# Paired stick-breaking heads, first weights in three pieces with norm sums beside the steps, and linear attention scores in row halves

## The reference, cut to what matters

```python
x += 0.5 * post(SwiGLU_1(pre(x)))          # D_MODEL 1024, D_FF 2816
h  = pre(x) @ w_in                         # GLA q, k, v, gate, low rank | SB q, k, v
# stick-breaking heads (8, dh 64), strictly causal:
z = q k^T / 8 + bias
log_stay = where(valid, log_sigmoid(-z), 0)
after = reverse_cumsum(log_stay) - log_stay
w = where(valid, exp(log_sigmoid(z) + after), 0);  o = w v
# gated linear attention (4 heads, dk 64, dv 128), exact decays between every two tokens
att[t,s] = sum_d q[t,d] k[s,d] exp(b[t,d] - b[s,d]);  o = att v + (q exp(b)) S
x += post(concat(rms(o_gla) * silu(gate), rms(o_sb)) @ w_out)
x += 0.5 * post(SwiGLU_2(pre(x)))
x += post(sigmoid(pre(x) @ W_g) * (p @ W_up))
```

## Time and profile before

| | |
|---|---|
| median of 3 runs | 1417.98 us (1417.67 to 1421.84) |
| the profiled execution's own time | 1419.12 us |
| its span, first to last instruction | 1417.4 us |
| granted TensorE clock, mean share of full | 0.942 |
| busy: PE, DVE, ACT, POOL | 1297.7, 606.0, 412.9, 151.1 us |

### The profile page before, as it was taken

How to read it: one execution, slowest core, us unless ns; L and a number is a source line. 1 busy time by engine, 2 the same in 40 slices (tenths; PEclk the granted TensorE clock), 3 DMA queues, 4 the chain that set the end, 5 groups by cost and what they waited for, 6 DMA issues and landing times.

```text
span 1417.4 us, 22180 instructions
## 1 busy us (share of the span) xinstructions
PE 1297.7 (92%) x9420; PEld 1226.5 (87%) x9420; DVE 606.0 (43%) x631; ACT 412.9 (29%) x462; POOL 151.1 (11%) x167
## 2 busy tenths in 40 slices
PE   5999999999986999979979869589999999999883
PEld 4999999999985999957647649589999999999883
DVE  5344412444337222345467641744442134433744
ACT  5222222222234111244321063432222222222442
POOL 6200000000013000010023301300000000001321
PEclk9999999999997999979967869899999999999997
DMA  5222223222331222211500102112222322222201
GB/s 184 89 89 81 68 89 119 61 88 67 91 109 32 87 89 92 90 47 46 163 30 17 32 16 90 60 58 78 79 78 80 104 90 89 78 75 88 87 31 64
DMA packets 36743, 109.98 MB, mean 78 GB/s; under 512 B 4626, under 2 KB 4642, under 8 KB 36562
## 3 DMA queue, kind: packets, MB, share of 16 engines
q1 hardware_dynamic: 34850, 103.10, 22.3%
q0 software_dynamic: 1232, 5.01, 1.1%
q10 hardware_dynamic: 608, 1.10, 0.2%
HBM read 103.57 MB, written 5.64 MB: 77 GB/s over the span
## 4 chain that ended last, share of the span: by engine, by line
PE 86%; DVE 8%; ACT 3%; issue 1%; POOL 1%; DMA 0%; ACTq 0%; POOLq 0%; DVEq 0%
PE PS L431 73%; PE PS L699 2%; DVE work L1135 2%; DVE a_lo L1126 1%; DVE x L1147 1%; PE PS L553 1%; PE PS L582 1%; PE PS L538 1%; PE PS L442 1%; PE PS L757 1%; PE PS L562 1%; PE PS L579 1%; PE PS L728 1%; PE PS L760 1%; DMA gate_w<-in_gate_w 0%
## 5 line engine op out<-in xcount | busy, mean ns | idle before, releaser
L431 PE MATMUL PS<-a_hi,w_hi 128*128 128x272 f32 (+1 forms) x2064 | 435.8, 292 | 49.8 <-DVE a_lo L1126 23.8
L431 PE MATMUL PS<-a_hi,w_lo 128*128 128x272 f32 (+1 forms) x2064 | 434.1, 292 | 0.0
L431 PE MATMUL PS<-a_lo,w_hi 128*128 128x272 f32 (+1 forms) x2064 | 431.1, 291 | 0.0
L431 PEld LDWEIGHTS PS<-a_hi,w_hi 128*128 128x128 f32 (+1 forms) x2064 | 327.9, 190 | 57.7 <-issue 32.2
L431 PEld LDWEIGHTS PS<-a_hi,w_lo 128*128 128x128 f32 (+1 forms) x2064 | 328.0, 190 | 0.5
L431 PEld LDWEIGHTS PS<-a_lo,w_hi 128*128 128x128 f32 (+1 forms) x2064 | 326.8, 190 | 0.5
L1120 DVE TENSOR_TENSOR w_lo<-raw,w_hi 128x2048 fp32r<-128x2048 f32 (+2 forms) x97 | 201.8, 2081 | 231.5 <-ACT w_hi L820 231.5
L820 ACT ACTIVATE w_hi<-raw 128x2048 fp32r<-128x2048 f32 (+2 forms) x97 | 166.0, 1711 | 116.9 <-PE PS L431 116.8
L431 PE MATMUL PS<-h_hi,w_hi 128*128 128x272 f32 x704 | 146.1, 289 | 0.0
L431 PE MATMUL PS<-h_lo,w_hi 128*128 128x272 f32 x704 | 145.2, 287 | 0.0
L431 PE MATMUL PS<-h_hi,w_lo 128*128 128x272 f32 x704 | 145.0, 287 | 0.0
(11 more groups left out here) (283 smaller groups left out, 1041.9 us busy)
## 6 DMA issues: line engine op xcount, KB each, us to landing
raw<-in_f_in SPq DMA_DIRECT2D x86, 512.0 KB, 4.4
raw<-in_f_out SPq DMA_DIRECT2D x32, 384.0 KB, 3.5
raw<-in_w_in SPq DMA_DIRECT2D x24, 512.0 KB, 4.6
raw<-in_f_out SPq DMA_DIRECT2D x32, 320.0 KB, 3.1
raw<-in_w_out SPq DMA_DIRECT2D x8, 512.0 KB, 4.8
y<-in_cache_sb_k SPq DMA_DIRECT2D x16, 256.0 KB, 2.8
raw<-in_ple_w_gate SPq DMA_DIRECT2D x8, 512.0 KB, 4.3
x<-in_x SPq DMA_DIRECT2D x8, 272.0 KB, 7.0
```

What stands on the lines that cost most here:

```text
L431: last = mm(PS[0:width, 4 * quad + 2 * c + half, 0:HALF], wt[:, slot, cols], act[:, k, half * HALF:(half + 1) * HALF], start=(k == 0 and n ...
```

## The change

Three edits are made together.

1. **Start and norm sums.** Step 0's weights come in three pieces (columns 0 to 511, 512 to 1023, 1024 to 2047) with a semaphore each; `bias`, `gate_w` and the page table move to SP behind x and step 1; the wait at the start is for `vec` alone. The squares of the first norm go to the eight tiles of `y`. A norm sum has no ticket any more. It goes to banks 2 and 3 of a quad. At the head of a stage, PE does tile 0 of step 1 (banks 0 and 1), then the sum, waits until ACT's Ln has read it (`sum_free`), and does tile 1 of step 1.
2. **Paired heads.** `q_pad` is gone. The logits of two heads are made together from rows 0 to 63 and 64 to 127, alternately, into different banks, in three units u per pair p (diagonal blocks; the rest of key block 0; the rest of blocks 1 and 2), over four banks in turn. Six `sb_z` buffers replace two and also hold the weights. The pages of the samples ride at the end of units. `prompt_out` runs once per pair with the two heads' 64-column halves alternately.
3. **Linear attention.** Every level has one matmul of 64 rows and 128 columns per head and chunk, the two heads alternately, into one bank each. `q_lev` has no zero half, and DVE makes it in one instruction of 128 rows.

```diff
@@ sum_norm
-                t = sum_ticket[j]
-                open_t(t)
+                t, quad = sum_after[j], sum_after[j] % 2
+                pe.wait_ge(psum_free[quad], t // 2 + 1)
+                if j:
+                    pe.wait_ge(sig["sum_free"], j)
                 pe.wait_ge(sig["sq_used"], 8 * (j + 1))
@@ product
                 body(Step(0), ready)
-                if norm is not None:
-                    sum_norm(norm)
-                steps(pe, 1, n, body)
+                st = Step(1)
+                t, quad, use = ticket(st, name)
+                weights(W0[name] + 1)
+                open_ticket(t, quad, use)
+                dense(quad, st.parity(W0[name]), tiles, n_k, rhs, only=0)
+                sum_norm(norm)
+                pe.wait_ge(sig["sum_free"], norm + 1)
+                dense(quad, st.parity(W0[name]), tiles, n_k, rhs, only=1).then_inc(sig["psum_full"], 1)
+                steps(pe, 2, n, body)
@@ start, ACT
-            act.wait_ge(sig["vec_in"], 16 * 3)
+            for c0, c1, landed in FIRST:
+                act.dma_start(raw[:, 0, c0:c1], a["f1_in"][0][:, c0:c1]).then_inc(landed, 16)
+            act.wait_ge(sig["vec_in"], 16)
             for k in range(KD):
                 act.wait_ge(sig[f"x_in{k}"], 16)
-                input_tile(k, "f1_pre", 0)
...
+                c = VEC["f1_pre"] + k
+                fn(a_hi[:, k, :], flat(x[:, k]), ACT.Copy, scale=vec[:, c:c + 1]).then_inc(sig["a_hi_ready"], 1)
+                if k < 3:
+                    c0, c1, landed = FIRST[k]
+                    act.wait_ge(landed, 16)
+                    fn(w_hi[:, 0, c0:c1], raw[:, 0, c0:c1], ACT.Copy).then_inc(sig["first_hi" if k < 2 else "split_hi"], 1)
+                fn(flat(y[:, k]), flat(x[:, k]), ACT.Square).then_inc(sig["sq_ready"], 1)
@@ heads, PE
+            def prompt_z(p, u):
+                n = 3 * p + u
+                banks_ = ((0, 1), (2, 7))[n % 2]
+                if n >= 2:
+                    pe.wait_ge(sig["z_out"], n - 1)
...
+                for col, j, q0, q1 in blocks:
+                    for hh in range(2):
+                        r = slice(64 * hh, 64 * hh + 64)
+                        last = mm(PS[:, banks_[hh], col:col + q1 - q0], k_[r, j * P:(j + 1) * P], q_[r, q0:q1],
+                                  start=True, stop=True)
+                for at_, b in unit_pages(p, u):
+                    last = page_z(b, PS[:, banks_[at_], 384:448])
+            for p, u in ((0, 0), (0, 1), (0, 2), (1, 0)):
+                prompt_z(p, u)
+            pe.wait_ge(sig["setup_new"], 1)
+            prompt_z(1, 1)
+            for p in range(pairs):
+                prompt_sums(2 * p)
+                if p + 1 < pairs:
+                    prompt_z(p + 1, 2)
+                if p:
+                    prompt_out(p - 1)
+                prompt_sums(2 * p + 1)
+                if p + 2 < pairs:
+                    prompt_z(p + 2, 0)
+                    prompt_z(p + 2, 1)
+            prompt_out(pairs - 1)
@@ level, PE
-                        last = mm(PS[:, b0 + c // 2, col:col + 256].rearrange("p (h t) -> p h t", h=2), k_[:, tok],
-                                  q_[:, :, tok], start=True, stop=True)
+                for c in range(N_CH):
+                    tok = slice(c * P, (c + 1) * P)
+                    for hh, r in enumerate(rows_):
+                        last = mm(PS[:, b0 + hh, tok], k_[r, tok], q_[r, tok], start=True, stop=True)
@@ level_q, DVE
-                for hh in range(2):
-                    r = slice(64 * hh, 64 * hh + 64)
-                    ins = v.tensor_tensor(upper(q_lev[m % 2][:, hh, :]), upper(gq[p]), upper(decay[m % 2]), ALU.mult)
+                ins = v.tensor_tensor(upper(q_lev[m % 2]), upper(gq[p]), upper(decay[m % 2]), ALU.mult)
@@ chunk_states, PE
-                for hh in range(2):
-                    for c in range(N_CH):
+                for c in range(N_CH):
+                    for hh in range(2):
```

More of the change, by code:

```diff
@@ L419, in weights, with dense @@
                 pe.wait_ge(sig["split_lo"], w + 1)
-            def dense(quad, slot, tiles, n_k, rhs, ready=None, stride=None, width=P):
-                stride = stride or tiles * width
+            def dense(quad, slot, tiles, n_k, rhs, ready=None, width=P, only=None):
+                stride = tiles * width
                 for k in range(n_k):
@@ L426, in dense @@
                         ready(k)
-                    for c in range(tiles):
+                    for c in range(tiles) if only is None else (only,):
                         cols = slice(k * stride + c * width, k * stride + (c + 1) * width)
@@ L897, in ffn @@
                 if name == "f1":
-                    split(Step(0), "in", T0["f1_post"])
+                    split(Step(0), "in", T0["in"])
                 else:
@@ L1079, in _ @@
             fn(p_hi[:], p_raw[:], ACT.Copy).then_inc(sig["p_hi_ready"], 1)
-            split(Step(0), "f2_up0", T0["out_post"])
+            split(Step(0), "f2_up0", T0["f2_up0"])
             norm(3)
@@ L1274, in _ @@
+            pairs = SB_HEADS // 2
+            masked(0)
             magnitudes(0)
+            magnitudes(1)
             softplus(0, sb_z[0], sb_s[0])
-            for h in range(SB_HEADS):
-                if h + 1 < SB_HEADS:
-                    magnitudes(h + 1)
-                exponents(h)
-                if h + 1 < SB_HEADS:
-                    softplus(h + 1, sb_z[(h + 1) % 2], sb_s[(h + 1) % 2])
-                if h >= 1:
-                    head_out(h - 1)
-            head_out(SB_HEADS - 1)
+            softplus(1, sb_z[1], sb_s[1])
@@ new lines, in _ @@
+            masked(1)
+            for p in range(pairs):
+                exponents(2 * p)
+                if p + 1 < pairs:
+                    magnitudes(2 * p + 2)
+                if p >= 1:
+                    pair_out(p - 1)
+                if p + 1 < pairs:
+                    softplus(2 * p + 2, sb_z[(2 * p + 2) % 6], sb_s[0])
+                exponents(2 * p + 1)
+                if p + 1 < pairs:
+                    magnitudes(2 * p + 3)
+                if p + 2 < pairs:
+                    masked(p + 2)
+                if p + 1 < pairs:
+                    softplus(2 * p + 3, sb_z[(2 * p + 3) % 6], sb_s[1])
@@ L1287, in _ @@
+            pair_out(pairs - 1)
             new = slice(0, N_SAMPLE)
```

324 lines of the change are left out of this document (156 added, 168 removed).

## The result

| | before | after |
|---|---|---|
| median of the runs beside each other | 1418.81 (1417.67 to 1421.84, 4 runs) | 1401.53 (1399.07 to 1402.37, 4 runs) |
| ratio | | 0.9874, 95% interval 0.9859 to 0.9889 |
| span of the profiled execution | 1417.4 | 1399.7 |

The change makes the kernel faster, by 1.3%: 17.9 us by the ratio of 1419 us, 17.3 by the two medians. The forecast was 1387 us with a range of 1376 to 1400. The direction was right; the size was forecast at 31 us, and the time lies 1.5 us above the range.

A forecast was written before the change was run, and what follows sets the result against it. PE was taken to bound the heads, PE and DVE together the levels. Start and norm sums 9.7, heads 13.2 and levels 8.5 made 31.4 us off 1419.1, 1387.7, stated as a median of 1387; range 1376 to 1400.

The forecast's parts named there:

- `f1_up0` and `in`: Start and norm sums: step 2 begins 3.9 us earlier in `f1_up0` and 4.9 us earlier in `in`.
- heads: Prompt heads: paired row halves run at once on PE and save 13.2 us, bounds 5 to 16.
- levels: Linear attention: shorter PE levels and one `level_q` instruction less on DVE save 8.5 us, bounds 3 to 12.
- `f2_up0` and `gate`: Norm sums there: step 2 begins 1.6 us earlier in `f2_up0` and 0.7 us later in `gate`.
- The new wait for `w_lo` of step 2: Feed-forward stages: step 2 waits about 2 us for its weights, which ACT splits only behind the norm.
- the stretch is then DVE's: Levels, 740 to 765: PE's 23.5 us shrink to about 18, DVE's 23.4 to 20.4, so DVE bounds.
- 8 of stalls: Heads: PE waits 1.2 us at `sums(2)`, 2.6 at `sums(6)`, 0.9 at `sums(7)`, 3.3 at the last output.
- one of the prediction's own signs of being wrong: Heads: the prediction is wrong if the granted clock there is under 0.9.
- The first one: Rival: pairs overlap only in part or shape changes cost double; 18 us gained in all, 1400 us; chance 0.15.
- the changes of shape: Heads: some 12 more changes of tile shape on PE, about 0.2 us each at full clock, 2.4 us.
- The sums' delay: Rival: new gaps before step 2 drop the clock, sums give 2 us, total 1394; within the forecast's 0.63.
- if the clock fell throughout the heads: Rival: gaps and half-filled passes bring all PE work in the heads to half clock; about +15 us, 1433; chance 0.04.

The follow-up runs named there:

- e6: e4 with each level's products in turn, the four of head 0 and then the four of head 1, in all 16 levels; 1412.31 us.
- e9: e6 with each level product on all 128 rows instead of 64, so the linear attention is not the reference's; 1392.36 us.
- e11: The kernel before with the paired heads alone; 1409.28 us.
- e1: The kernel before with the start and norm sums part alone (step 0 in three pieces, sums in two banks, norms beside the steps); 1412.85 us.
- e4: The changed kernel with the split of step 2's weights moved ahead of the norm on ACT and DVE, in four stages; 1388.41 us.
- e8: e4 with a unit's second batch of page products issued ahead of the unit's own logits; 1385.03 us, ratio 0.9784.

## Why the prediction was right in direction and wrong in size

Of 31.4 us forecast in the profiled execution 17.7 came. By the stages (each against the kernel before):

| step | forecast | profile after | what the runs show |
|---|---|---|---|
| `f1_up0` and `in` | -8.8 | -6.6 | -6.5, mean of three against three |
| heads | -13.2 | -9.4 | -11.1, mean of eight (100.4) against three (111.5) |
| levels | -8.5 | -3.1 | -2, mean of five (103.7) against six (105.7); timed 0.9 to 6.2 |
| `f2_up0` and `gate` | -0.9 | +1.4 | +0.6, means 602.6 and 602.0 |
| sum | -31.4 | -17.7 | -19.0; timed -17.9 |

**Right.** The new wait for `w_lo` of step 2, with its place and length: the forecast put step 1 of `f1_up0` at 24.9 (24.92) and step 2 at 40.9 (41.36). The 24.9 is luck in part: the first `a_hi` begins at 4.05, within the bounds of the landing, not at 5.4, and from there to the end of `w_lo` of step 1 it is 20.8 us, not 19.5 (that `w_lo` begins at 21.43 and takes 3.44 us, not 2.28; POOL's adds run until 22.7). In `in` no low clock followed the sum (1.00 in the row at 463), which gives nearly all of its part. Two heads' outputs take 2.3 us as worked out, a level 1.16 and 2.08 us (1.2 and 2.2). DVE does not bound the heads. `gate` is slower: from step 2 of `f2_up0` to step 2 of `gate` it is 425.5 us (924.63 to 1350.10), where the forecast's figures for the kernel before give 424.3.

**Wrong: the levels.** The step that failed is "the stretch is then DVE's". It took the clock of the earlier trace rows over (0.91, 0.86) and cut only the passes. In the changed kernel the clock is 0.64 and 0.66 there, and PE stays the bound: busy 23.17 of 25 us, where about 18 were forecast, with DVE at 20.16 as forecast. The levels gave 2 us by the stages for 8.5. e6 and e9 show that half the rows go with the lower clock. By the Trainium skill (TensorE: Matmul & The Clock Gate, Part 1) the gate follows how busy the PE has been; the prediction weighed that rule for the heads alone, and left open how a pass on half the rows counts. e6 does not agree with the rule if a pass on half the rows counts as busy in full: busy 96% of its stretch (34.51 of 36.04 us) and at 0.51.

**Too large: the heads.** The work was right. In the 81.7 us of the row the mean clock of 0.86 costs 11.4 us against a full one; the forecast had 3.0 for its one set of sums at half clock (7.3 for 4.3), so some 8.4 us are clock. PE idles 5.65 us where I had 8 of stalls: 2.4 back. 75 + 8.4 - 2.4 = 81.0, and from 607.40 to 688.03 it is 80.6. `sums(0)` came 4.8 us earlier against the kernel before where 3.2 were forecast (11.4 less the 6.6 of the start). The term that was mis-sized is the clock in the heads; a clock under 0.9 there was one of the prediction's own signs of being wrong, and it was 0.86. Over the eight profiles of the new heads the shortfall is some 2 us, so the profile of the changed kernel caught one of the dearer executions; but e11's profile is the fastest of its six runs, 5.0 us under their median, and by the timed runs the heads alone give 9.2 us, 4 under the forecast.

**Small: behind the gaps.** Forecast nothing for the clock behind the new waits of 2 us in `f1_up0` and `gate`; it fell in the profile after (0.70, 0.72) and cost 1.7 each (0.30 x 5.6 and 0.28 x 6.0), and in `f1_up0` not in e1. The prediction had this among its rivals, for all stages, `in` included; in `in` and in `f2_up0` it did not happen.

**The rivals.** None came true as it stood. The first one's 1400 is near the 1401.53 in number only: the halves do overlap, and what the levels and part of the heads lost is clock; what the changes of shape cost was not taken apart. The sums' delay took part of their gain, not nearly all of it (6.8 us of 9.7 came by e1, where 2 would have been left). The range was cut off at the centre of the first rival, 1400, where it had to reach beyond it. Two sums of the prediction are wrong without bearing on its forecast: if the clock fell throughout the heads, 60 us more against 31.4 of gains are about +29 and 1447, not +15 and 1433; and 37.05 us of ACT over 7.7 heads, with the 0.2 each, are 10.0 us per pair, not 11.6.

## What to carry to other kernels

A change that makes TensorE's passes fewer or narrower has to be priced with the clock that it will get, not the one of the trace before: price it once at the old clock and once at half, and hold the range to both. Where a wait is taken away, follow what stood behind it in program order: here two splits of weights, moved ahead of the norm, gave 12.9 us on top of the 17.9 of the change itself. The kernel to keep is e4 (1388.41 us), with e8 (1385.03) level with it.

## What was not expected of the hardware

- With the level products on 64 of 128 rows, PE was busy 96% of the second pair's levels and granted 0.51, nearly throughout the 1.2 GHz level; with them on 128 rows, busy 94%, 0.86. Nothing else differs in the two kernels' code. The 128-row products against half-zeroed queries, the old form, kept 0.91 and 0.86, so rows that multiply zeros seem to count as rows in use.
- The same code in the same place runs at different clocks in different executions: 96.9 to 103.1 us for the heads, 0.94 to 0.87; and a wait of 2.1 us is followed by 0.70 once and by 1.00 another time. A single profile carries some 3 us of such chance to either side in a stage of 100 us, while the medians of the kernel before, in its four groups of runs, lie between 1418.32 and 1420.22 us.
